# The layer norms' reciprocal root as one power of -0.5 on GpSimd, in place of a square root on ScalarE and a reciprocal with one refinement step on VectorE

## What is computed

```python
def layer_norm(x, g, b):
    mu = mean(x); xc = x - mu
    var = mean(xc * xc)
    return xc * rsqrt(var + 1e-5) * g + b
...
h = layer_norm(ALPHA * x + mixer(x))
r = relu(h @ w1)
x = layer_norm(ALPHA * h + (r * r) @ w2 + (p @ ple_w) * sigmoid(h @ gate_w))
```

## Time and profile before

| | |
|---|---|
| median of three runs | 2200.69 us |
| profiled execution, its own time | 2200.9 us |
| its span (first to last instruction) | 2199.1 us |
| TensorE matmul busy | 2130.7 us, 97% |
| VectorE busy | 1255.0 us, 57% |
| ScalarE busy | 807.3 us, 37% |
| GpSimd busy | 70.3 us, 3% |
| mean granted TensorE clock | 0.99 |

### The profile page before, as it was taken

How to read it: one execution, slowest core, us unless ns; L and a number is a source line. 1 busy time by engine, 2 the same in 40 slices (tenths; PEclk the granted TensorE clock), 3 DMA queues, 4 the chain that set the end, 5 groups by cost and what they waited for, 6 DMA issues and landing times. The chain is left out here.

```text
span 2199.1 us, 31589 instructions
## 1 busy us (share of the span) xinstructions
PE 2130.7 (97%) x13166; PEld 2113.8 (96%) x13166; DVE 1255.0 (57%) x1823; ACT 807.3 (37%) x1233; POOL 70.3 (3%) x61
## 2 busy tenths in 40 slices
PE   8999999999999999999999999998989999999996
PEld 8999999999999999999999999998989999999996
DVE  4233367786454444445676777876755355444576
ACT  3122123654333222323444455455333224233343
POOL 0000000000000000000110030002000000000000
PEclk9999999999999999999999999999999999999998
DMA  4011141343132111111212434442213112122232
GB/s 168 29 57 39 56 134 65 113 134 125 55 106 77 39 57 40 46 51 39 68 68 70 129 115 150 136 134 70 77 55 96 58 49 66 53 75 77 77 116 99
DMA packets 51455, 179.67 MB, mean 82 GB/s; under 512 B 7936, under 2 KB 8064, under 8 KB 51328
## 3 DMA queue, kind: packets, MB, share of 16 engines
q1 hardware_dynamic: 49248, 177.72, 24.4%
q10 hardware_dynamic: 2080, 0.12, 0.1%
HBM read 173.36 MB, written 4.46 MB: 81 GB/s over the span
## 5 line engine op out<-in xcount | busy, mean ns | idle before, releaser
L616 PE MATMUL ps<-h_hi,w_split 128*128 128x352 f32 x2160 | 700.0, 324 | 4.8 <-DVE h_lo L921 2.1
L618 PE MATMUL ps<-h_hi,w_split 128*128 128x352 f32 x2160 | 692.8, 321 | 0.0
L617 PE MATMUL ps<-h_lo,w_split 128*128 128x352 f32 x2160 | 692.2, 320 | 0.0
L616 PE MATMUL ps<-r_hi,w_split 128*128 128x352 f32 x1632 | 536.5, 329 | 37.5 <-DVE acc L1046 37.5
L618 PE MATMUL ps<-r_hi,w_split 128*128 128x352 f32 x1632 | 528.3, 324 | 0.0
L617 PE MATMUL ps<-r_lo,w_split 128*128 128x352 f32 x1632 | 527.8, 323 | 0.0
L1046 DVE TENSOR_TENSOR acc<-acc,ps 128x352 f32<-128x352 f32 x768 | 376.4, 519 | 145.1 <-PE ps L618 143.9
L549 DVE TENSOR_TENSOR w_split<-w_raw,w_split 128x1024 fp32r<-128x1024 f32 x294 | 357.0, 1232 | 136.4 <-ACT w_split L727 135.7
L727 ACT CAST w_split<-w_raw 128x1024 fp32r<-128x1024 f32 x294 | 301.6, 1046 | 322.1 <-PE ps L618 316.5
L616 PEld LDWEIGHTS ps<-h_hi,w_split 128*128 128x128 f32 x2160 | 405.0, 187 | 7.6 <-issue 3.7
L617 PEld LDWEIGHTS ps<-h_lo,w_split 128*128 128x128 f32 x2160 | 406.4, 188 | 1.1
(11 more groups left out here) (80 smaller groups left out, 1118.2 us busy)
## 6 DMA issues: line engine op xcount, KB each, us to landing
w_raw<-w_stream SPq DMA_DIRECT2D x318, 512.0 KB, 3.5
x_raw<-x_t SPq DMA_DIRECT2D x6, 704.0 KB, 8.4
y_t<-acc SPq DMA_DIRECT2D x4, 704.0 KB, 4.1
w_raw<-p_t SPq DMA_DIRECT2D x6, 352.0 KB, 2.9
y_t<-acc SPq DMA_DIRECT2D x4, 352.0 KB, 2.4
pool_new<-acc ACTq DMA_DIRECT2D x2, 60.0 KB, 7.2
vec<-vectors SPq DMA_DIRECT2D x1, 78.0 KB, 7.2
pool_history<-pool_hist SPq DMA_DIRECT2D x1, 60.0 KB, 6.7
```

Of the source, the lines that this page charges most:

```text
L616: pe.matmul(out, wh, mov_h, start=first, stop=False)
L617: pe.matmul(out, wh, mov_l, start=False, stop=False)
L618: return pe.matmul(out, wl, mov_h, start=False, stop=last)
```

## The change

The `rstd` row and the Newton step go. `var` still adds epsilon and copies to SBUF on VectorE; then GpSimd raises it to the power of -0.5, with a constant column that it set at the start. The waits that stood on `std_done` go with it.

```diff
@@ def norm(i, done):
         rows = [(0, 3.2, [("sum", n, done)]), (2, 3.1, [("mean", n)]), (1, 0, [("square", n)]), (1, 3.2, [("vsum", n)]), (2, 0.6, [("var", n)]),
-                (1, 4.0, [("rstd", n)]), (1, 3.1, [("norm", n)]), (1, 0, [("affine", n, 0)]), (1, 0, [("affine", n, 1)])]
+                (1, 3.1, [("norm", n)]), (1, 0, [("affine", n, 0)]), (1, 0, [("affine", n, 1)])]
...
-        std, _ = place("std", [P, TG], F32, at - -(-TG * 4 // 32) * 32)
+        powers, _ = place("minus_half", [P, 1], F32)
...
@@ ScalarE, side
-                elif what == "var":
-                    act.wait_ge(var_copied, i + 1)
-
-                    wait(act, rstd_done, i)
-                    act.activation(std[:], var[:], ACT.Sqrt).then_inc(std_done, 1)
...
@@ VectorE, side ("finish" calls the same parts)
                 elif what == "vsum":
                     dve.wait_ge(squared, i + 1)
 
-                    wait(dve, rstd_done, i)
+                    wait(dve, var_full, i)
...
-                elif what == "rstd":
-                    dve.wait_ge(std_done, i + 1)
-                    wait(dve, normed, i)
-                    then(dve.reciprocal(std[:], std[:]))
-
-                    then(dve.scalar_tensor_tensor(out=rstd[:], in0=std[:], scalar=-0.5, in1=std[:], op0=ALU.mult, op1=ALU.mult))
-                    then(dve.tensor_tensor(rstd[:], rstd[:], var[:], ALU.mult))
-                    dve.scalar_tensor_tensor(out=rstd[:], in0=rstd[:], scalar=1.5, in1=std[:], op0=ALU.add,
-                                             op1=ALU.mult).then_inc(rstd_done, 1)
@@ GpSimd
+            pool.memset(powers[:], -0.5).then_inc(powers_set, 1)
...
+            def root(i):
+
+                pool.wait_ge(var_copied, i + 1)
+                wait(pool, normed, i)
+                pool.tensor_tensor(rstd[:], var[:], powers[:].to_broadcast([P, TG]), ALU.pow).then_inc(rstd_done, 1)
+
+            pool.wait_ge(powers_set, 1)
             for step in plan:
 
                 for what, i, *rest in step.side:
                     if what == "fill":
                         window_sums(i)
+                    elif what in ("var", "finish"):
+                        root(i)
```

More of the change, by code:

```diff
@@ L447, in bass_streaming_trunk @@
         s_mean, _ = place("sum_mean", [P, TG], F32)
-        s_var, at = place("sum_var", [P, TG], F32)
-        std, _ = place("std", [P, TG], F32, at - -(-TG * 4 // 32) * 32)
+        s_var, _ = place("sum_var", [P, TG], F32)
+        powers, _ = place("minus_half", [P, 1], F32)
         var, _ = place("var", [P, TG], F32)
@@ L483, in bass_streaming_trunk @@
         mean_sum, var_sum, mean_full, var_full = (sem(n) for n in ("mean_sum", "var_sum", "mean_full", "var_full"))
-        centred, squared, var_copied, std_done, rstd_done, normed, affine, ln_hi, h_ready, ln_step = (
-            sem(n) for n in ("centred", "squared", "var_copied", "std_done", "rstd_done", "normed", "affine", "ln_hi", "h_ready",
+        centred, squared, var_copied, powers_set, rstd_done, normed, affine, ln_hi, h_ready, ln_step = (
+            sem(n) for n in ("centred", "squared", "var_copied", "powers_set", "rstd_done", "normed", "affine", "ln_hi", "h_ready",
                              "ln_step"))
@@ L767, in side @@
                         act.activation(blk(squares, n, k), blk(acc, n, k), ACT.Square).then_inc(last_squared, 1)
-                    side("var", i)
                     for k in range(KD):
@@ L948, in side @@
                     side("var", i, GRP_BANK)
-                    side("rstd", i)
                     dve.wait_ge(rstd_done, i + 1)
```

## The result

The changed kernel takes 2791.14 us (median of 4 runs, 2783.2 to 2792.82), the kernel before 2201.04 us in the same session. The ratio is 1.2672, 95% interval 1.2656 to 1.2689: 590 us slower. It lies far above the forecast of 2226 us and above the range.

A forecast was written before the change was run, and what follows sets the result against it. TensorE, busy 97%, was taken as the bound up to norm 11. End 3.5, blocks 23.6 and clock 6, less relief 8, added 25.1 us to 2200.9: 2226 us, with a range of 2188 to 2320.

The forecast's parts named there:

- the term P: Length of GpSimd's power over 352 columns, once per norm: taken as 8 us, bounded between 0.8 and 16.8.
- The Trainium skill's rule: Dependent fp32 operations on GpSimd cost 4 cycles an element each at 1.2 GHz; 24 over 352 columns estimated at 28 us.
- third rival: A long power, over 12 us: 2277 us at 12, 2335 us at 16.8; chance 18%.
- the blocks: Norms 0 to 10: the power stops VectorE's first two-SBUF-input instruction behind var and its queue; 23.6 us reach TensorE.
- clock: TensorE at 1.2 GHz behind new waits, about 1.2 us each; 6 us added for five.
- the end: Norm 11: the 4.6 us chain becomes the power plus about 0.1 us handover, 3.5 us later at 8 us.
- held port: VectorE instructions with two SBUF inputs don't run while a GpSimd instruction reads SBUF; basis of the 2226 us forecast.
- the relief: Norms 0 to 10: rstd leaves VectorE and norm moves earlier, so TensorE waits less; 8 us taken of 9.7.
- second rival: It comes out even: power of 5.4 to 6.2 us, or a long one freeing the port early; 2200 us, 16%.
- three signs of being wrong: Power outside 6.2 to 12 us, instructions beside it keeping their length, or a 5 us block leaving TensorE untouched.
- The wait of `norm`: norm also waits for the power, but stands 3.9 us or more behind var within the same block; not priced again.
- The table loads: ScalarE's 15 loads of 1.28 us, 19 us in all, go without Sqrt; costed at nothing, at most 19 us gain.

The follow-up runs named there:

- e11_free: e1_mult with a power over 48 columns, some 8 us, on GpSimd in norms 0, 1, 2, 9 and 10; 2182.5 us, ratio 0.9924.
- e10_hold: e1_mult with five more GpSimd multiplies of 764 columns ahead in norms 0, 1, 2, 9 and 10; 2199.9 us, ratio 0.9995.
- e2_cols48: Changed kernel with the power over 48 of the 352 columns, the rest of rstd constant 1; 2195.2 us, ratio 0.9963.
- e1_mult: Changed kernel with a GpSimd multiply in place of the power, so the root is left out; 2175.5 us, ratio 0.9866.
- e3_late: Changed kernel with the multiplication of norms 2, 3, 8 and 9 planned 15 steps behind var instead of 1; 2591.2 us, ratio 1.1753.
- e8_plan: e1_mult with an empty row of cost 4.0 in rstd's place, so all norms keep their old places; 2186.2 us, ratio 0.9936.

## Why the prediction was wrong

**The size of one term decided all.** The step that failed is the cost of the power, the term P under "What is added": its upper bound, "some twelve multiply-adds each, and each as dear as a whole pass", gave 16.8 us, and "I take P = 8" set the sum. Measured: 56.42 us, seven times the value taken and 3.4 times the upper end. The bound was made of a number of steps that no row gave. The Trainium skill's rule that I set aside (GPSIMD Engine Reference, Performance pitfalls for Q7 kernels) gave an estimated 28 us by the same count of steps, nearer but still half. With the measured 56.42 the third rival's terms give 11 x 53.4 - 35.1 = 552 for the blocks, 13 of clock, 51.9 at the end, less 8: 2810 us, 19 more than measured. That nearness is in part luck: the blocks were reckoned by a held port, which the traces contradict, and the terms miss both ways (545 for the blocks less the relief, where TensorE's waits grew by 514; 13 for the clock, where its work grew by 24). And the range had no place for so long a power: I gave "over 12 us" 18% and cut the range at 15.6 us.

**The mechanism had a wrong half.** "Each power blocks the first VectorE instruction with two SBUF inputs behind `var`" until it ends: that is false for the power. A split beside it takes 1.23 us, in the changed kernel and in e11_free, and the instruction that starts just behind the power's start in norms 1 and 7 is stretched by 0.24 us and not by 56. Beside additions and the multiplies of e10_hold such instructions are indeed stretched. I had put this as the second rival ("a long power reads its operands early and lets go of the port"), and at P = 8 that rival gave 2200 us; e2_cols48, the same case at 8.01 us, measured 2195.2, while the held-port sum gave 2226. That the rival came so near is luck in part: against e1_mult TensorE waits 11 us longer in e2_cols48, where the rival had 3 for `norm`'s wait, and the relief was larger than its 8. Why the power leaves the port free was not tried. Two of the prediction's own three signs of being wrong came true: P outside 6.2 to 12, and instructions beside the power that keep their length. Since `norm` waits over the same stretch, a power of 56 us costs nearly the same by either mechanism, and the total alone could not have told them apart.

**The wait of `norm`** was named but "isn't priced again". It is the whole cost beside the products: 542.6 us in eleven waits, and moving four of them took 200 us off (e3_late).

**The end** was right in form: P and a handover of 0.1 us, 56.53 us measured for 56.42.

**The relief** was too small: 10 us beside the products and 3.7 at the end for the shortest power, 2187 us; e1_mult measured 2175.5, so 21 to 25 us beside the products, by the median or the ratio. The step behind ("steps behind also shift, and where the shift puts another long instruction ahead of a `down` step a wait can come up") was right that places matter and wrong on the sign: by e8_plan the new places were worth 11 to 15 us.

**The table loads** at nothing: not refuted, not settled by the times (4 us by the medians, 9 by the ratios, with intervals that overlap); the waits of TensorE differ by 1.7 us. "No table load but the first" was off by one: 2 loads are left of 16, at 0.74 and 437.88 us.

**The clock**: 1.2 us behind each wait was forecast; the 24.2 us of longer TensorE work are some 2.2 us for each of the eleven waits, if all of it is the clock's.

## What to carry to other kernels

An elementwise instruction of a kind that the trace doesn't show has no price: 1 us and 50 us are both open until one is run alone, over two widths, which also tells the fixed part from the slope. Before a slow function is put on any engine, ask how many distinct numbers it works on; here 352 columns held one number each on all partitions, and 4 columns of 88 partitions hold as many, though the matmuls that turn them round cost most of the gain. And in a queue worked through in order, the consumer's place costs as much as the producer's length: a long instruction is free where its reader stands far enough behind.

## What the runs showed of the hardware

GpSimd's power takes 159 ns a column and 0.4 us fixed, within some 1 us whatever the number of partitions (1, 16, 128), the exponent (-0.5 or 2.0) and the value (1.3 or 4096); over 352 columns that is 56.42 us, 73 times a multiply (0.773 us). VectorE's instructions with two SBUF inputs keep their length beside it (1.23 us for a split) but for some that start in its first 1.1 us (0.77 for 0.53, 1.53 for 1.22, 2.19 for 1.62 us), and are stretched beside GpSimd's multiplies (4.07 for 2.36 us). An fp32 matmul record of one moving column lasts 0.21 to 0.28 us on TensorE and adds 0.09 to 0.15 us of busy time. Behind each of the eleven waits of 38.6 to 50.9 us TensorE's granted clock was 0.50 (1.2 GHz) at first and 1.00 a few us later (behind norm 2's, 12 matmul records in 3 us against 27 in 4 us afterwards).
